# Modulation tiles summed over their rows by VectorE, ScalarE and GpSimd, with TensorE adding over partitions only

## The reference, cut to what matters

```python
def hybrid_layer(x, y, c_silu, cc_silu, ada_w, ada_b, norm_w, w_in, ..., need_ctx):
    shift_x, scale_x, gate_x = jnp.split((c_silu @ ada_w + ada_b)[:, None, :], 3, axis=-1)
    shift_y, scale_y, gate_y = jnp.split(cc_silu @ ada_w + ada_b, 3, axis=-1)
    hx = rms_norm(x, norm_w) * (1.0 + scale_x) + shift_x
    hy = rms_norm(y, norm_w) * (1.0 + scale_y) + shift_y
    ...   # projections of hx and hy by w_in, three attention branches
    x = x + gate_x * merge_branches(...)
    if need_ctx:              # the first layer only
        y = y + gate_y * merge_branches(...)
```

## Time and profile before

| | |
|---|---|
| median of 3 runs | 1955.73 us |
| lowest, highest | 1950.49, 1956.59 us |
| the profiled execution | 1955.3 us |
| its span from the first to the last instruction | 1953.6 us |
| TensorE busy | 1934.3 us, 99% |
| VectorE busy | 1244.9 us, 64% |
| ScalarE busy | 914.4 us, 47% |
| GpSimd busy | 340.1 us, 17% |
| weights and other data read | 286.49 MB, 147 GB/s |

### The profile page before, as it was taken

One profiled execution on the slowest core, in us unless ns is written; L12 is line 12 of the kernel. 1 busy time (PEld: TensorE's weight loads), 2 busy tenths in 40 slices (PEclk: granted clock), 3 DMA queues, 4 the chain that ended last, 5 costly groups with the idle time before them and its releaser, 6 DMA issues.

```text
span 1953.6 us, 32393 instructions
## 1 busy us (share of the span) xinstructions
PE 1934.3 (99%) x12094; PEld 1661.3 (85%) x12094; DVE 1244.9 (64%) x1910; ACT 914.4 (47%) x1435; POOL 340.1 (17%) x326
## 2 busy tenths in 40 slices
PE   8999999999999999999999999999999999999998
PEld 6777878777787788998899888998888888998887
DVE  5554443354533655556667886799877886679874
ACT  5444222244432544435555554775544554555553
POOL 1000100111121000301113320004312330203320
PEclk9999999999999999999999999999999999999999
DMA  8222343412233332343355555455556555545553
GB/s 317 90 74 65 130 153 133 146 65 66 68 110 130 130 103 87 101 159 108 110 180 178 191 185 192 148 169 192 184 192 205 185 191 185 172 156 182 191 184 117
DMA packets 79435, 289.27 MB, mean 148 GB/s; under 512 B 8912, under 2 KB 9168, under 8 KB 79312
## 3 DMA queue, kind: packets, MB, share of 16 engines
q1 hardware_dynamic: 77760, 282.13, 43.2%
q0 software_dynamic: 1120, 4.72, 0.8%
q10 hardware_dynamic: 432, 0.72, 0.1%
HBM read 286.49 MB, written 1.05 MB: 147 GB/s over the span
## 4 chain that ended last, share of the span: by engine, by line
PE 90%; issue 8%; ACT 1%; DVE 1%; POOL 0%; DVEq 0%; POOLq 0%; ACTq 0%
PE bank L2618 24%; PE bank L2611 15%; PE bank L2612 13%; PE bank L2613 13%; PE bank L2624 13%; PE bank L2852 2%; PE bank L2835 2%; PE bank L2821 2%; PE bank L2892 1%; PE bank L2682 1%; PE bank L2877 1%; PE bank L2666 1%; PE bank L2742 1%; PE bank L2913 0%; POOL stats L1597 0%
## 5 line engine op out<-in xcount | busy, mean ns | idle before, releaser
L1994 DVE TENSOR_TENSOR w_lo<-raw,w_hi 128x1024 fp32r<-128x1024 f32 x484 | 625.8, 1297 | 251.5 <-ACT w_hi L1700 241.5
L1700 ACT ACTIVATE w_hi<-raw 128x1024 fp32r<-128x1024 f32 x484 | 508.7, 1056 | 432.9 <-PE bank L2624 212.8
L2611 PE MATMUL bank<-h,w_hi 128*128 128x512 f32 (+1 forms) x1312 | 465.6, 355 | 3.4 <-DVE w_lo L1994 1.5
L2612 PE MATMUL bank<-h,w_hi 128*128 128x512 f32 (+1 forms) x1312 | 444.6, 339 | 0.0
L2613 PE MATMUL bank<-h,w_lo 128*128 128x512 f32 (+1 forms) x1312 | 444.1, 338 | 0.0
L2618 PE MATMUL bank<-h,w_hi 128*128 128x512 f32 x1408 | 357.1, 393 | 0.5 <-issue 0.3
L2611 PEld LDWEIGHTS bank<-h,w_hi 128*128 128x128 f32 x1312 | 248.6, 190 | 58.3 <-issue 30.2
L2618 PEld LDWEIGHTS bank<-h,w_hi 128*128 128x128 f32 x1408 | 253.4, 189 | 46.9 <-DVE h L2152 0.5
L2613 PEld LDWEIGHTS bank<-h,w_lo 128*128 128x128 f32 x1312 | 248.9, 190 | 28.2
L2612 PEld LDWEIGHTS bank<-h,w_hi 128*128 128x128 f32 x1312 | 249.4, 190 | 21.8
L2624 PEld LDWEIGHTS bank<-h,w_lo 128*128 128x128 f32 x1408 | 193.7, 190 | 13.5
(11 more groups left out here) (257 smaller groups left out, 2299.1 us busy)
## 6 DMA issues: line engine op xcount, KB each, us to landing
raw<-in_weights SPq DMA_DIRECT2D x516, 512.0 KB, 3.3
early<-in_first SPq DMA_DIRECT2D x10, 512.0 KB, 13.3
bias<-in_rpb POOLq DMA_DIRECT2D x8, 384.0 KB, 3.4
early_o<-in_first SPq DMA_DIRECT2D x4, 512.0 KB, 16.3
x<-in_tokens SPq DMA_DIRECT2D x3, 512.0 KB, 7.1
work<-in_first SPq DMA_DIRECT2D x2, 512.0 KB, 15.7
out<-cols_out SPq DMA_DIRECT2D x4, 256.0 KB, 2.8
con<-in_consts SPq DMA_DIRECT2D x1, 544.0 KB, 18.0
```

Source lines behind the costliest of these rows:

```text
L1700: nc.scalar.activation(w_hi[:, n % SPLIT, :], raw[:, t % RAW, :], ACT.Copy).then_inc(hi_ready, 1)
L1994: dve.tensor_tensor(w_lo[:, t % RAW, :], raw[:, t % RAW, :], w_hi[:, SPLIT_NO[t] % SPLIT, :].bitcast(F32), ALU.subtract).then_inc(lo_ready, 1)
L2611: nc.tensor.matmul(dst, w_hi[:, SPLIT_NO[t] % SPLIT, at], hi, start=start, stop=False, skip_group_check=shared)
L2612: nc.tensor.matmul(dst, w_hi[:, SPLIT_NO[t] % SPLIT, at], lo, start=False, stop=False, skip_group_check=shared)
```

## The change

The 32 modulation tiles are no longer multiplied by TensorE. They are laid beside the jobs of the neighbourhood and retention groups, one per job and two at every seventh, from the second group's key job on (28 jobs). For each tile, three engines do the following at the beginning of its job, behind the split for a later job and behind the evacuation of the job before:

- VectorE multiplies the tile by the image tokens' factor of each row (one scalar per partition) and adds it to a running sum of 128 x 1024 in `m` ("sum" in what follows).
- ScalarE multiplies it by the context tokens' factor into `merge_tanh` or `square` ("product"), for the first three sections only: the last gate's context half isn't used. The first tile of a section goes directly to the sum's place.
- GpSimd adds the product to a second running sum in `m` ("add"), 21 times in all.

After the eighth tile of a section TensorE adds the sums over the partitions (`ada_fold`): a matrix `pick` with one column of ones serves as weights, and 8 matmuls of 256 columns (4 in the last section) write what the old code had in the bank. `ada_turn` follows as before. The job beside which a tile lies tells SyncE that both slots are free, at its end, and TensorE waits for the sums and products before the job's last block. The scheme of the ring makes the split of a projection tile come one job ahead in this part. GpSimd's bias loads keep their place in the list, and a wait of two of them for `ada_set` goes away.

```diff
-ADA_BESIDE = [(0, 2), (1, 0), (1, 1)]
-ADA_LAST = (1, 2)
-ADA_SLOTS = [0] * 4 + [2, 0] * 12
+ADA = [(0, 2), (1, 0), (1, 1), (1, 2)]
+ADA_SLOTS = [0] * 4 + [2, 1, 1, 1, 1, 1, 1] * 4
+ADA_CTX = 3
...
+        beside = []
+        while blocks == KC and self.tile + len(beside) + 1 < NT and TILES[self.tile + len(beside) + 1][0] == "ada":
+            beside.append(self.tile + len(beside) + 1)
...
         self.flush()
+        job.u = [self.ada_sum(t) for t in beside]
...
+        for st in job.u:
+            if st.k == KC - 1:
+                self.later(3, lambda st=st: self.ada_fold(st.c))
...
+    def ada_fold(self, section):
+
+        u = self.add("ada_fold", c=section, t_use=self.use("T"))
+        self.later(1, lambda: self.add("ada_turn", u=u, layer=ADA[section][0], c=ADA[section][1]))
...
-        if layer == 0 and dc % 2:
-            for k in (dc - 1, dc):
-                ada_tile(s, ADA_LAST, k)
...
-                if st.layer and st.c < 2:
-                    pool.wait_ge(ada_set, sections[1, 1])
                 pool.dma_start(bias[:, slot, :, :], rpb[st.layer, st.c]).then_inc(bias_landed[slot], 16)
```

GpSimd's step:

```diff
+            def ada_sum_step(st):
+
+                if st.c >= ADA_CTX or st.k == 0:
+                    return
+                pool.wait_ge(ada_ctx, st.n + 1)
+                if ctx_adds(st):
+                    pool.wait_ge(ada_added, ctx_adds(st))
+                v = ada_sums(st.c, 1)
+                pool.tensor_tensor(v, v, ada_product(st), ALU.add).then_inc(ada_added, 1)
```

ScalarE's step (its head left out):

```diff
+            def ada_sum_step(st):
...
+                if st.k and ctx_adds(st) >= 2:
+                    act.wait_ge(ada_added, ctx_adds(st) - 1)
+                act.wait_ge(raw_landed[st.tile % RAW], 16 * (st.tile // RAW + 1))
+                dst = ada_product(st) if st.k else ada_sums(st.c, 1)
+                nc.scalar.activation(dst, raw[:, st.tile % RAW, :], ACT.Copy, scale=c_silu[:, st.k, 1:2]).then_inc(ada_ctx, 1)
```

VectorE's step, and TensorE's waits, release and folds:

```diff
+            def ada_sum_step(st):
+
+                c = c_silu[:, st.k, 0:1]
+                tile, v = raw[:, st.tile % RAW, :], ada_sums(st.c, 0)
...
+                if st.k == 0:
+                    dve.tensor_scalar(v, tile, c, None, ALU.mult).then_inc(ada_x, 1)
+                    return
+                dve.wait_ge(ada_x, st.n)
+                dve.scalar_tensor_tensor(out=v, in0=tile, scalar=c, in1=v, op0=ALU.mult, op1=ALU.add).then_inc(ada_x, 1)
...
+                    if i == KC - 1 and job.u:
+                        pe.wait_ge(ada_x, job.u[-1].n + 1)
+                        pe.wait_ge(ada_ctx, min(job.u[-1].n + 1, ADA_CTX * KC))
                     ins = three(dst, (job.tile, st.base + i), hi, lo, start=(i == 0), stop=(i == job.blocks - 1))
                 if st.at + st.part == job.blocks:
-                    ins.then_inc(half_used if job.first_half else tile_used, 1)
+                    ins.then_inc(half_used if job.first_half else tile_used, 1 + len(job.u or []))
...
-            def ada_tile_step(st):
...
-                for g in range(4):
-                    ins = nc.tensor.matmul(T[u.t_use % 2][32 * g:32 * g + 32, 0:SEQ], c_silu[:, k, :], columns[:, g, :, :],
-                                           start=(k == 0), stop=(k == KC - 1), skip_group_check=True)
...
+            def ada_fold_step(st):
+
+                conds = 2 if st.c < ADA_CTX else 1
+                pe.wait_ge(pick_set, 2)
+                pe.wait_ge(ada_x, KC * (st.c + 1))
+                if conds == 2:
+                    pe.wait_ge(ada_added, (KC - 1) * (st.c + 1))
...
+                for j in range(conds):
+                    columns = ada_sums(st.c, j).rearrange("p (k g q) -> p g k q", k=KC, g=4)
+                    for g in range(4):
+                        ins = nc.tensor.matmul(T[st.t_use % 2][32 * g:32 * g + 32, 0:SEQ], pick[:, 31 - j:63 - j],
+                                               columns[:, g, :, :], start=(j == 0), stop=(j == conds - 1),
+                                               skip_group_check=True)
```

More of the change, by code:

```diff
@@ L66, in tile_order @@
     for layer in range(DEPTH):
-        ada = [("ada", *section, k) for section in ADA_BESIDE for k in range(KC)] if layer == 0 else []
+        ada = [("ada", *section, k) for section in ADA for k in range(KC)] if layer == 0 else []
         slots = list(ADA_SLOTS) if layer == 0 else [0] * len(ADA_SLOTS)
@@ L77, in tile_order @@
             for n, name in enumerate(("nk", "nv", "nq", "ng")):
-                out.append((name, layer, c))
+                out += beside((name, layer, c))
         for h in range(4):
@@ L93, in tile_order @@
             out.append(("w_out", layer, n))
-            if layer == 0 and n % 2:
-                out += [("ada", *ADA_LAST, k) for k in (n - 1, n)]
     for layer in range(DEPTH):
@@ L605, in schedule_layer @@
         s.background = softmax_units(g)
-    ada = [(section, k) for section in ADA_BESIDE for k in range(KC)] if layer == 0 else []
-    slots = list(ADA_SLOTS) if ada else [0] * len(ADA_SLOTS)
-    def ada_tiles():
-        count = slots.pop(0)
-        for section, k in ada[:count]:
-            ada_tile(s, section, k)
-        del ada[:count]
     for h in range(4):
@@ L729, in schedule_layer @@
             norm_part(s, norm, 0)
-        if layer == 0 and dc % 2:
-            for k in (dc - 1, dc):
-                ada_tile(s, ADA_LAST, k)
-    return norm
-def ada_tile(s, section, k):
-    if k == 0:
-        s.section = Step("section", s.count("section"), layer=section[0], c=section[1], t_use=s.use("T"))
-    s.flush()
-    if section != ADA_LAST or k < KC - 2:
-        s.split_ahead(s.tile)
-    s.add("ada_tile", tile=s.tile, u=s.section, k=k)
-    s.tile += 1
-    if k == KC - 1:
-        done = s.section
-        done.tile = s.tile - 1
-        s.later(1, lambda: s.add("ada_turn", u=done))
+    return norm
 def new_norm(s, cols, how=None, weight=None, adds="pool"):
```

89 lines of the change are left out of this document (50 added, 39 removed).

## The result

| | before | changed |
|---|---|---|
| median of six runs each | 1955.15 us | 1963.86 us |
| lowest, highest | 1950.49, 1956.59 | 1960.49, 1965.88 |
| the profiled execution | 1955.3 us | 1965.88 us |
| its span | 1953.6 us | 1964.1 us |

The ratio is 1.0043, 95% interval 1.0033 to 1.0054: slower by 0.43%, beyond the 0.3% that was set as the bound of a difference. The time lies in the range (1944 to 1966), 6.9 us above the forecast of 1957.0, and it is the case of piled-up waits (1965). By that bound it is the outcome "slower", to which the prediction gave 0.26.

A forecast was written before the change was run, and what follows sets the result against it. TensorE's instructions were taken to bound the kernel. 1955.3 - 18.2 (old matmuls) + 4.5 (folds) + 8.0 (value jobs) + 6.9 (key jobs, first retention head) = 1956.5, as median 1957.0 us; range 1944 to 1966.

The forecast's parts named there:

- piled-up waits: Rival: waits of ScalarE, VectorE and TensorE on GpSimd's queue pile up, 19.6 us or more, time 1965; chance 0.25.
- slower: Outcome of a time above 1961.6 us, over 0.3% slower than before; chance 0.26.
- gain of 13.7 us: On TensorE alone: 18.2 us of old modulation matmuls gone, less 4.5 us for the new folds.
- What leaves TensorE: Old modulation matmuls, 16 pairs: fifteen at 1.21 us give 18.1 us, the last 0.1; 18.2 us gone.
- The collision: VectorE and GpSimd share SBUF ports, so a sum that finds an add under way waits up to 2.4 us.
- race: In the value jobs GpSimd's add starts 0.3 us before VectorE's sum could, so the sum waits.
- four value jobs: Value jobs with a softmax and an add: TensorE waits 2.0 us in each, 8.0 us together.
- key jobs and first retention head: Late softmax chains: 0, 2.3 and 2.7 us in three groups' key jobs, 1.9 in the head; 6.9 together.
- query and gate jobs I count at nothing: No wait in query and gate jobs; in the query job 3 us of room cover a blocked sum.
- that wait once, at 0.9 us: TensorE's new wait before the eighth block of the third group's key job, 0.9 us within the chain's delay.
- 0.1 us, not 1.2: Sixteenth pair, in the norm's tail after w_out: removing it gains only 0.1 us, as TensorE then waits for ScalarE's square.
- Hidden collisions: Rival: with a product 0.3 us longer or a shifted phase, sums come first and collisions miss TensorE; 1945, chance 0.33.

The follow-up runs named there:

- e8: Changed kernel, but VectorE sums both columns behind the job's first softmax step and SyncE waits for the sums instead of TensorE; 1942.8 us.
- e1: Changed kernel without GpSimd's 21 additions, so the context sum stays incomplete; 1943.3 us.
- e5: Changed kernel with sums, products and additions in place, but SyncE instead of TensorE waits for sum and product; 1960.1 us.
- e6: Changed kernel with sum, product and addition behind the job's first softmax step, and SyncE waiting instead of TensorE; 1944.2 us.
- e10: Changed kernel with only VectorE's sum moved late, product and addition still ahead, and SyncE waiting instead of TensorE; 1947.4 us.
- e12: Changed kernel with GpSimd's additions cut to 256 of 1024 columns, all waits kept, context sum incomplete; 1944.0 us.
- e11: e8 plus six matmuls of 128 columns with unused result in the norm's tail behind w_out; 1943.1 us.
- e4: Changed kernel, but VectorE sums both columns behind the job's first softmax step, with TensorE still waiting for the sums; 1995.5 us.

## Why the prediction was right and where it failed

**Bound and sign of each part: right.** TensorE's own instructions set the time and its waits are lost in full. The gain of 13.7 us was real: e8 and e1 stand 0.8 and 1.3 us above the 1942.0 that the sum gives for a kernel without new waits (1941.6 and 0.4); e8's four runs lie between 1939.3 and 1945.8, so it is confirmed to about 3 us. The kernel is slower because the waits cost more than that.

**What leaves TensorE: right.** Aligned by their order, the matmuls of the two traces close up by 0.95 to 1.35 us at each of fifteen places where a pair stood, 17.5 us in sum for 18.1. The folds took 1.1 us for the first one (134.72, the next block at 135.72), some 3.9 for all, where I took 4.5.

**The collision: right in mechanism and in its race.** In the value job of the third group GpSimd's addition began at 109.67 and VectorE's sum at 109.85:

```profile
109.67 2.39 POOL L1558 TENSOR_TENSOR m<-m,square 128x1024 f32<-128x1024 f32 x1 [6.38 <-ACT square L1715]
```

```profile
109.85 3.29 DVE L2099 SCALAR_TENSOR_TENSOR m<-raw,c_silu,m 128x1024 f32<-128x1024 f32 x1
113.07 0.75 DVE L2317 TENSOR_TENSOR bank<-bank,bias 128x256 f32<-128x256 f32 x2
```

The margin is 0.18 us, and it is 0.17 to 0.27 in all four value jobs; 0.3 was predicted. Sums of 1.27 us became 3.2 to 3.5, additions took 2.4 as predicted, and up to 3.4 behind a split, which I hadn't priced. The rule of the Trainium skill that the prediction cites (SBUF — State Buffer, section "Who interferes with whom") held in this trace: the sum with two SBUF operands ended 1.08 us after the addition did. The product's step was 1.04 us (108.44 to 109.48) for the 1.0 of the prediction, too little to decide anything.

**The waits, place by place.**

| | predicted | measured |
|---|---|---|
| four value jobs | 8.0 (2.0 each) | 4.9 (0.33, 0.94, 1.90, 1.73) |
| key jobs and first retention head | 6.9 (0, 2.3, 2.7, 1.9) | 6.3 (0, 2.32, 1.76, 2.26) |
| query and gate jobs | 0 | 2.7 (2.35, 0.19, 0.18) |
| later retention heads | not counted | 2.5 (1.33, 1.21) |
| sum | 14.9 | 16.5 |

Of the last, 0.75 us had been there before, so 15.8 are new. The sum came out well by luck, because two errors balanced. The value jobs cost less, since TensorE reaches the transpose late itself after the wait in the key job before: I added waits in neighbouring jobs as if they were independent. e5 shows the same from the other side, where 7 us of waits taken away brought 3.8. And the step "query and gate jobs I count at nothing" failed. In the first retention head's gate job the turn of a section stands behind a blocked sum, and it frees the bank that the transposes need:

```profile
207.16 3.29 DVE L2099 SCALAR_TENSOR_TENSOR m<-raw,c_silu,m 128x1024 f32<-128x1024 f32 x1
210.37 0.44 DVE L2108 STREAM_TRANSPOSE m<-bank 128x256 f32<-128x256 f32 x1
```

In the retention heads it is not the softmax chain but the eighth block itself, which waits for a blocked sum (3.42 and 3.31 us). I had priced that wait once, at 0.9 us.

**What was missing: the clock, and TensorE's start behind a wait.** The sum took every us of TensorE's work at the rate of the kernel before. Against the profiled execution it is 9.4 us short (1956.5 to 1965.9):

| term | us |
|---|---|
| waits, 15.8 instead of 14.9 | 0.9 |
| two falls of the clock behind waits (104.3 and 155.5), 3.4 us each at half rate | 3.3 |
| the norm's tail: 0.6 lost where 0.1 was to be gained | 0.7 |
| the start, which ran 17.1 us at half rate and not 6.8 | 2.6 |
| pairs 0.6 less and folds 0.6 less than priced | 0 |
| left over | 1.9 |

The start belongs to the single execution and not to the change (below). Against the median, 6.9 us, it drops out, and the others with the rest make 6.8. What is left over is the start behind each wait. With the two traces aligned, the matmul behind a wait is later by 0.15 us more than the idle time explains (at 77.89 us 0.33 of idle and 0.48 of delay, at 210.96 us 2.35 and 2.51), and where it is the first of a projection block the next one by another 0.11. Over 13 places that is some 2.8 us, an estimate; 0.9 us of it are missing again in the total because the distance between the two executions shrinks behind 700 us (11.4 to 10.6), the cause of which is open. The falls' cost is shown by the distances of the starts (0.43 for 0.23 us). That they hang on the waits is supported by e1, e6, e8, e10 and e12, whose waits are 2.0 us at most and where none is left between 30 us and the norm's tail; it is not a fixed rule, as the waits without a fall show.

In the tail the sixteenth pair was the step "0.1 us, not 1.2". It did fill a gap, as I said, but without it the clock fell there too (in the profiled executions of all kernels without the pair but e11 and e12). In the changed kernel the matmuls behind the gap run at the lower level:

```profile
659.53 1.05 PE L2779 MATMUL bank<-con,square 128*128 128x1 f32 x8 [0.84 <-ACT square L1736]
660.45 1.90 PE L2704 MATMUL bank<-con 128*128 128x128 f32 x8
662.14 1.95 PE L2826 MATMUL bank<-con,stats 128*128 128x128 f32 x8
```

**The rivals.** "Hidden collisions", 1945, was refuted for this kernel: it named a product longer by 0.3 us as its condition, and the product was longer by 0.04, so the add kept its lead. "Piled-up waits", 1965, came nearest in time, with the retention heads' 1 to 2 us (2.5 measured), but the waits stayed at 15.8, below the 19.6 from which it was to decide, and its other condition, ScalarE held up by GpSimd, never occurred. What carried the time out of the forecast's 1952 to 1962 was the clock and TensorE's start behind the waits, which no case named. The range of 1944 to 1966 held since it was wide enough to take in the rival; the forecast's mechanism was right, its time of 1957 was not.

## What to carry to other kernels

Work that is moved to an idle engine costs what stands in front of somebody's deadline: here 1.3 us ahead of the softmax chain fitted its room and cost 1.3 us in sum (e1), 2.5 us or more cost 11 to 22 us in sum, whether it was a blocked instruction, two bare ones, or a blocked split and a bare sum. So put it behind the step that someone waits for, and let the engine that really needs its result (here SyncE, for the buffer) wait for it, not the one that sets the time. The version so built, e8, computes everything and is 0.7% faster than the kernel before (0.9932, 0.9911 to 0.9952).

Waits of the bottleneck are not independent terms: one that is taken makes the next smaller and can make the work behind it slower.

## What was not expected of the hardware

In the changed kernel TensorE's granted clock fell to its lower level, 1.2 GHz, for 3.4 us at the end of a wait of 2.3 us and 0.3 us behind one of 1.9 us; each fall cost about 1.6 us beyond the wait. Before the first TensorE had been busy for 1.12 of 3.30 us, before the second for 1.60 of 3.50. Behind waits of 1.76, 1.73 and 2.35 us in the same trace it did not fall. In e4, with waits of up to 6.1 us, the clock fell nine times between 60 and 270 us, three of them for 6.8 us.

The start of the kernel ran at the lower level for anything from nothing (e10) to 17.1 us (the changed kernel) in the profiled executions, with the same instructions there. Over 52 executions of the kernel before the mean granted clock and the time go together: 1951.1 us on average in the six at 0.998 and 0.999, 1956.5 in the 22 at 0.995, 1958.1 in the three at 0.993. Most of the spread from 1950 to 1959 us goes with it. That it arises at the start is likely and not shown: in the one trace of the kernel before, the lower level stands at the start (6.8 us) and in the last 9 us. The Trainium skill (TensorE: Matmul & The Clock Gate, Part 1: The HAM clock gate) calls the low rate the default which activity releases, and its release variable from run to run; the start agrees with it, and a comparison of two profiled executions has to take it out first.
